# Shared-key attention with scores laid out by keys for the exponential and by queries for the maximum

## The reference

```
def gqa_attention(q, k, v):          # q, k were normed and rotated
    scale = HEAD_DIM ** -0.5
    def block(j, qb):
        logits = jnp.einsum("bqhgd,bkhd->bhgqk", qb, k).astype(jnp.float32) * scale
        p = jax.nn.softmax(logits, axis=-1).astype(v.dtype)
        return jnp.einsum("bhgqk,bkhd->bqhgd", p, v)
...
o = gqa_attention(q, concat([kc, k]), concat([vc, v]))     # 512 queries, 768 keys
oc = gqa_attention(qc, kc, vc) if need_ctx else None       # 256 queries, 256 keys; layer 0 only
x = x + gt * ((o * silu(z)) @ w_out)
```

## Time and profile before

| | us |
|---|---|
| median of 3 runs | 3264.06 |
| lowest and highest | 3261.76, 3265.40 |
| profiled execution, device time | 3259.84 |
| its span | 3258.0 |
| TensorE, VectorE, ScalarE, POOL busy | 3124.7, 1493.2, 1305.8, 1122.0 |
| granted TensorE clock, mean | 0.987 |

### The profile page before, as it was taken

One profiled execution on the slowest core, in us unless ns is written; L12 is line 12 of the kernel. 1 busy time (PEld: TensorE's weight loads), 2 busy tenths in 40 slices (PEclk: granted clock), 3 DMA queues, 4 the chain that ended last, 5 costly groups with the idle time before them and its releaser, 6 DMA issues. The chain is left out here.

```text
span 3258.0 us, 50609 instructions
## 1 busy us (share of the span) xinstructions
PE 3124.7 (96%) x20584; PEld 2577.8 (79%) x20584; DVE 1493.2 (46%) x2748; ACT 1305.8 (40%) x2383; POOL 1122.0 (34%) x614
## 2 busy tenths in 40 slices
PE   9989999999989999999999999999999998799999
PEld 7757788887667888888887888887888777688787
DVE  5952443218744344242476410246333349843473
ACT  4352333223533333232466213267223248723463
POOL 4532444446414444433111222242224422125212
PEclk9999999999999999999999999999999999999999
DMA  4355222324452323222000121110122200013102
GB/s 166 112 182 175 84 97 97 100 86 138 161 189 79 99 95 113 95 81 87 21 2 21 59 65 59 59 44 15 59 67 88 79 20 1 8 52 116 40 2 78
DMA packets 83878, 259.92 MB, mean 80 GB/s; under 512 B 11968, under 2 KB 17472, under 8 KB 83648
## 3 DMA queue, kind: packets, MB, share of 16 engines
q1 hardware_dynamic: 83648, 256.69, 23.8%
HBM read 239.34 MB, written 2.10 MB: 74 GB/s over the span
## 5 line engine op out<-in xcount | busy, mean ns | idle before, releaser
L188 PE MATMUL ps<-hs,head 128*128 128x512 f32 (+1 forms) x4176 | 864.3, 364 | 17.2 <-DVE hs L1068 6.8
L188 PE MATMUL ps<-hs,WS 128*128 128x512 f32 (+1 forms) x4176 | 855.1, 362 | 7.9 <-POOL WS L169 7.8
L188 PEld LDWEIGHTS ps<-hs,head 128*128 128x128 f32 x4176 | 711.9, 189 | 158.1 <-issue 13.4
L188 PEld LDWEIGHTS ps<-hs,WS 128*128 128x128 f32 x4176 | 710.6, 189 | 135.4 <-POOL WS L169 10.3
L169 POOL TENSOR_TENSOR WS<-W,WS 128x1024 fp32r<-128x1024 f32 x168 | 406.9, 2422 | 643.9 <-ACT WS L161 643.9
L169 POOL TENSOR_TENSOR head<-W,head 128x1024 fp32r<-128x1024 f32 x165 | 400.4, 2426 | 623.5 <-ACT head L161 623.5
L161 ACT CAST WS<-W 128x1024 fp32r<-128x1024 f32 x168 | 176.1, 1048 | 341.2 <-PE ps L188 315.1
L1846 ACT ACTIVATE prob<-ps,low 128x768 f32<-128x768 f32 (+4 forms) x320 | 223.6, 701 | 165.6 <-DVE low L1920 109.4
L161 ACT CAST head<-W 128x1024 fp32r<-128x1024 f32 x165 | 172.7, 1047 | 196.6 <-PE ps L188 196.5
L1355 PE MATMUL ps<-kk,qq 64*128 64x256 f32 (+3 forms) x2064 | 213.3, 333 | 25.8 <-ACT prob L1583 14.7
L1355 PEld LDWEIGHTS ps<-kk,qq 64*128 64x128 f32 x2064 | 156.5, 185 | 93.4 <-issue 41.4
(11 more groups left out here) (325 smaller groups left out, 3776.1 us busy)
## 6 DMA issues: line engine op xcount, KB each, us to landing
W<-in_stream_dram SPq DMA_DIRECT2D x433, 512.0 KB, 3.3
swap<-prj SPq DMA_DIRECT2D x168, 64.0 KB, 2.5
band<-in_bias_band_dram SPq DMA_DIRECT2D x8, 512.0 KB, 4.1
prj<-prj SPq DMA_DIRECT2D x64, 64.0 KB, 2.8
xT<-in_x_dram SPq DMA_DIRECT2D x4, 512.0 KB, 6.2
out_dram<-xT SPq DMA_DIRECT2D x8, 256.0 KB, 2.7
W<-in_stream_dram SPq DMA_DIRECT2D x1, 1536.0 KB, 10.9
xT<-in_ctx_dram SPq DMA_DIRECT2D x1, 1024.0 KB, 7.1
```

The source lines that it names most:

```text
L188: last = pe.matmul(out, a(i), b(j), start=start and n == 0, stop=stop and n == 2)
```

## The change

Only layers 0 and 3 take the new `attention_by_columns`. Work is now by steps: a step (g, j) is one block of 128 keys against the 512 queries of a pair. Scores are computed twice, with three products each. Once with keys on partitions (`score`): keys stationary, queries moving, and a fourth product that adds the negated maximum of each query (a matrix of ones times `shift`); the exponential of that can go as it is into the product with the values (`weigh`), with 512 columns moving. And once, a group ahead, with queries on partitions (`rank`), only to find the maximum (`largest`): 8 units of 128 queries and 384 keys, all in banks 0 and 1 after the first group. The maxima are turned once a group (`turn`) and laid out by `lay_shift`. Row sums are formed by POOL (the sum of two steps' probabilities, `pair`) and TensorE (`total`, ones in 32 columns, one strip of the array for each 128 queries), inverted by VectorE (`invert`, 128 x 128), spread by TensorE (`spread_inverse`) and applied by VectorE (`scale`) after the gate (`gate`). Context queries of two pairs form one group of 512 columns with two steps and two ranking units.

```
--- before.py
+++ after.py
@@ -1940,6 +1940,282 @@
+class Columns:
+    def __init__(self, groups):
+        self.groups = groups
+        self.steps = [(g, j) for g, (_, _, _, _, blocks) in enumerate(groups) for j in range(len(blocks))]
+        self.start = [0] + np.cumsum([len(blocks) for *_, blocks in groups]).tolist()
+        self.units_before = [0] + np.cumsum([len(self.units(g)) for g in range(len(groups))]).tolist()
+    def units(self, g):
+        n = len(self.groups[g][4])
+        return [(t, i) for t in range(4) for i in range(2)] if n == NT else [(0, 0), (2, 0)]
+    def units_at(self, g, j):
+        if g + 1 == len(self.groups):
+            return []
+        units, n = self.units(g + 1), len(self.groups[g][4])
+        at = range(1, n - 1) if n == NT else range(n)
+        return [u for i, u in enumerate(units) if at[i * len(at) // len(units)] == j]
+    def key_slot(self, g):
+        return self.groups[g][0] // 4
...
+def attention_by_columns(nc, M, C, operands, v_col, out, gate_tile):
...
+        prob, inv, sides = sb("prob", [P, 3, 2, S]), sb("inv", [P, P]), sb("sides", [P, 2, 32])
+        parts, low = sb("parts", [P, 2, 2, 4, 2]), sb("low", [P, 2, P])
+        pair = sb("pair", [P, 2, 2, S])
+        shift, ones, pick = sb("shift", [P, 2, S], F32R), sb("ones", [P, P], F32R), sb("pick", [P, 4])
...
+            @block.gpsimd
+            def _(pool):
...
+                for s, (g, j) in enumerate(steps):
+                    if j == 0 and g + 1 < G:
+                        pool.wait_ge(queries_high, g + 1)
+                        nc.gpsimd.tensor_tensor(place(q_at(g + 1, 1), g + 1), rows_of(M.prj, g + 1),
+                                                place(q_at(g + 1, 0), g + 1), ALU.subtract).then_inc(queries_low, 1)
+                    if s % 2:
+                        pool.wait_ge(exped, 2 * (s + 1))
+                        if s >= 5:
+                            pool.wait_ge(summed, s // 2 - 1)
+                        nc.gpsimd.tensor_tensor(pair[:, s // 2 % 2], prob[:, (s - 1) % 3], prob[:, s % 3], ALU.add
+                                                ).then_inc(paired, 1)
...
+            @block.tensor
+            def _(pe):
+                def rank(g, unit, bank):
+                    t, i = unit
+                    if len(groups[g][4]) == NT:
+                        pieces = [(0, t, 3 * P * i, 3 * P)]
+                    else:
+                        pieces = [(2 * P * x, t + x, S, 2 * P) for x in range(2)]
+                    for c, q, k, n in pieces:
+                        for x, (a, b) in enumerate(((0, 0), (1, 0), (0, 1))):
+                            for hd in range(2):
+                                last = pe.matmul(M.ps[:, bank + hd, c:c + n], q_at(g, a)[half(hd), q * P:(q + 1) * P],
+                                                 operands.kk[C.key_slot(g)][half(hd), b, k:k + n], start=x == 0,
+                                                 stop=x == 2)
+                    last.then_inc(ranked, 1)
+                def turn(g):
+                    if len(groups[g][4]) == NT:
+                        pe.wait_ge(lowered, g + 1)
+                    else:
+                        pe.wait_ge(maxed, C.units_before[g + 1])
+                    pe.transpose(M.ps[:, 0, 0:P], low[:, g % 2, :], M.const[:, C_ID:C_ID + P]).then_inc(turned, 1)
+                def score(s):
+                    g, j = steps[s]
+                    kb, kk = groups[g][4][j], operands.kk[C.key_slot(g)]
+                    if s >= 2:
+                        pe.wait_ge(exped, 2 * (s - 1))
+                    at = lambda hd: M.ps[:, 2 + 2 * (s % 2) + hd, :]
+                    for n, (a, b) in enumerate(((0, 0), (1, 0), (0, 1))):
+                        for hd in range(2):
+                            pe.matmul(at(hd), kk[half(hd), a, kb * P:(kb + 1) * P], q_at(g, b)[half(hd), :],
+                                      start=n == 0, stop=False)
+                    if j == 0:
+                        pe.wait_ge(shifted, g + 1)
+                    for hd in range(2):
+                        last = pe.matmul(at(hd), ones[half(hd), :], shift[half(hd), g % 2, :], start=False, stop=True)
+                    last.then_inc(scored, 1)
+                def weigh(s):
+                    g, j = steps[s]
+                    p, blocks = groups[g][0], groups[g][4]
+                    kb, first, final = blocks[j], j == 0, j == len(blocks) - 1
+                    pe.wait_ge(exped, 2 * (s + 1))
+                    if first and g:
+                        pe.wait_ge(gated, g)
+                    for hd in range(2):
+                        last = pe.matmul(M.ps[half(hd), 6, :], M.vtok[:, kb, v_col(p) + 64 * hd:v_col(p) + 64 * hd + 64],
+                                  prob[:, s % 3, hd, :], start=first, stop=final)
+                    last.then_inc(taken, 1)
+                def total(q):
+                    g, j = steps[2 * q]
+                    pe.wait_ge(paired, q + 1)
+                    if j == 0 and g:
+                        pe.wait_ge(scaled, g)
+                    for hd in range(2):
+                        for t in range(4):
+                            last = pe.matmul(M.ps[32 * t:32 * t + 32, 7, 0:P], sides[:, hd, :],
+                                             pair[:, q % 2, hd, t * P:(t + 1) * P], start=j == 0 and hd == 0,
+                                             stop=j == len(groups[g][4]) - 2 and hd == 1)
+                    last.then_inc(summed, 1)
+                def spread_inverse(g):
+                    pe.wait_ge(inverted, g + 1)
+                    for t in range(4):
+                        for hd in range(2):
+                            c = C_ID + 32 * t + 16 * hd
+                            last = pe.matmul(M.ps[half(hd), 7, t * P:(t + 1) * P],
+                                             M.const[:, c:c + 1].broadcast_to([P, 64]), inv[:],
+                                             start=True, stop=True)
+                    last.then_inc(spread, 1)
+                def sums(s):
+                    if s >= 3 and s % 2:
+                        total(s // 2 - 1)
+                    if s - 2 in C.start[1:]:
+                        spread_inverse(C.start.index(s - 2) - 1)
+                for n, unit in enumerate(C.units(0)):
+                    if n >= 3:
+                        pe.wait_ge(maxed, n - 2)
+                    rank(0, unit, 2 * (n % 3))
+                    keep_running(pe, M, 1, 7)
+                turn(0)
...
+                for s, (g, j) in enumerate(steps):
+                    score(s)
+                    n = len(groups[g][4])
+                    units = C.units_at(g, j)
+                    for unit in units:
+                        at = C.units_before[g + 1] + C.units(g + 1).index(unit)
+                        if unit == C.units(g + 1)[0]:
+                            pe.wait_ge(queries_low, g + 1)
+                            pe.wait_ge(shifted, g + 1)
+                            if g + 1 == second:
+                                pe.wait_ge(keys_low, 1)
+                        pe.wait_ge(maxed, at)
+                        rank(g + 1, unit, 0)
+                        if unit == units[0] and s:
+                            weigh(s - 1)
+                            sums(s)
+                    if not units:
+                        if j == n - 1 and n == NT and g + 1 < G:
+                            turn(g + 1)
+                        if s:
+                            weigh(s - 1)
+                            sums(s)
+                    if j == n - 1 and n < NT and g + 1 < G:
+                        turn(g + 1)
+                weigh(T - 1)
+                if T - 2 in C.start[1:]:
+                    spread_inverse(G - 2)
+                total(T // 2 - 1)
+                spread_inverse(G - 1)
...
+            def _(act):
...
+                    act.wait_ge(scored, s + 1)
+                    if s >= 3:
+                        act.wait_ge(taken, s - 2)
+                        act.wait_ge(paired, (s - 3) // 2 + 1)
+                    for hd in range(2):
+                        nc.scalar.activation(prob[:, s % 3, hd, :], M.ps[:, 2 + 2 * (s % 2) + hd, :], ACT.Exp
+                                             ).then_inc(exped, 1)
...
+                def largest(g, unit, bank):
+                    t, i = unit
+                    n = C.units_before[g] + C.units(g).index(unit)
+                    dve.wait_ge(ranked, n + 1)
+                    if len(groups[g][4]) == NT:
+                        dst, src = parts[:, g % 2, :, t, i], M.ps[:, bank:bank + 2, 0:3 * P]
+                    else:
+                        dst = low[:, g % 2, :].rearrange("p (h x) -> p h x", h=2)[:, :, t:t + 2]
+                        src = M.ps[:, bank:bank + 2, :].rearrange("p h (x n) -> p h x n", n=2 * P)
+                    v.tensor_reduce(dst, src, AX_X, ALU.max, negate=True).then_inc(maxed, 1)
```

(45 more changed lines are left out.)

46 lines of the change are left out of this document (added).

## The result

| | before | after |
|---|---|---|
| median, same chip | 3262.91 us (3258.34 to 3265.4, 4 runs) | 3402.05 us (3399.87 to 3404.39, 4 runs) |
| ratio, 95% interval | | 1.0421 [1.0409, 1.0434] |
| span of the profiled execution | 3258.0 | 3397.9 |
| layer 0's stage | 178.6 | 254.9 |
| layer 3's stage | 147.4 | 209.7 |

The change made the kernel 4.2% slower. A stage is taken here from the first load of its scores to the first load of the next stage. The two stages together grew from 326.0 to 464.6 us, 138.6 of the 139.9 us by which the spans differ. The rest of the program differs from execution to execution by some microseconds and is left alone. One execution of one variant took 4307 us at a mean granted clock of 0.74, in a slower state of the chip, and is left out of that variant's figures.

What follows compares the result with a forecast made beforehand. TensorE's streamed columns, changes of shape and waits for VectorE were taken as the bound: layer 3 +54.7, layer 0 +65.4, so 3259.8 + 120 = 3380, plus 4.2 to the median: 3384 us, range 3335 to 3430.

Steps and rivals of the forecast that it cites:

- The waits: TensorE idle for VectorE's reductions: 2.04 us behind the reciprocal, 1.86 behind the inverse's product, smaller ones; 5.68 a full group.
- A full group: Four works of a pair in layers 0 and 3: 19.70 us of TensorE plus waits, 25.4 against 17.55 before.
- rival 3: Totals: the four strips do not run together, 1.7 us instead of 0.43 each, time 3450; chance 0.05.
- rival 4: TensorE's clock falls to 1.2 GHz in the gaps, up to 17.5 us in each of 12 groups, up to 3594; chance 0.03.
- The start: Each stage's beginning: 10.0 us before the first block, with eight reductions in a row, then 18.3 for the rest of group 0.
- The contexts and the end: Layer 0's last part: three context groups of 11.1 us each, then 12.8 for the last one with the end.
- POOL's sum: Adding two blocks' probabilities: 2.42 us, up to 3.26; costed at nothing, with 8 us in all at the upper price.
- Rival 2: Weight loads are the bound in the two stages, fewer loads make the kernel faster, 3231 us; chance 0.03.
- The exchange: Per group on TensorE: 5.2 us of turning saved, spent on second scores (3.8), shift (1.3) and totals (1.3).
- 8R: Term for the eight ranking units' columns on TensorE in a full group: 4.32 us.
- Rival 1: VectorE's order costs nothing, reductions are done when ranking is due: 84 us less, 3300, still slower; chance 0.09.
- The signs: Expected profile after: groups of 25 us, reciprocal near 0.87, totals 0.43, VectorE near 50%, loads idle a fifth, clock 1.00.

Runs made afterwards that it cites:

- one ranking unit: Changed kernel with one of eight ranking units a full group kept, other maxima zero, queries scaled down 64 times: 3266.68 us, ratio 1.0008.
- reductions first: Changed kernel with VectorE taking the first reduction of each step before it gates, inverts or scales: 3339.8 us, ratio 1.0233.
- gaps filled: Changed kernel with three unread F32 matmuls of 256 columns put into each of the two long gaps of a full group: 3394.65 us, ratio 1.0397.
- one product in ranking: Changed kernel with the ranking maximum taken from the high-by-high product alone instead of three products: 3366.13 us, ratio 1.0302.

## Why the prediction was right, and where it was not

Forecast 3384, measured 3402: right in sign and inside the range, 18 us short. The mechanism, VectorE's order and the ranking chain, is what the experiments show; the nearness of the numbers is in part luck, as below.

- *The waits* came where they were listed, each released by a reduction. The loads' idle time of 2.16 and 1.90 us holds the change of shape too (0.20 and 0.17 where nothing is waited for), so 1.96 and 1.73 us compare with the sum's 2.04 and 1.86. TensorE started 0.05 us after VectorE's reduction (1632.37 + 0.90 = 1633.27, and 1633.32), not 0.15: the 0.14 of the earlier trace rows is ScalarE's. Taking the wait away by order alone gave 61 us of the 139.
- *A full group*: 25.4 forecast, 25.25 at full clock. The parts were less exact than the whole. The reciprocal took 0.96 us, not 0.87. The totals are 0.43 as forecast, so the strips run together and rival 3 is refuted, but I left out the change of shape between the product with the values and the totals, because no row of before had it. The Trainium skill, page "TensorEngine Tiling (Array Packing)", section Key Properties, has every change of tiling mode drain TensorE; the rows above agree, at 0.15 us. With 16 changes TensorE alone needs about 20.1 us, and the waits are 5.2, not 5.7 (20.1 is an estimate from the sum's prices). Two errors of half a microsecond cancelled; that the whole came out so near was luck.
- *The clock* was the largest error. I gave rival 4 a chance of 0.03, since gaps of 1.44 us had kept 1.00 and mine were to be "2.0". That reading was wrong as well: 1.44 is the idle time of the weight loads. In the start of layer 0's stage before, TensorE itself had nothing under way for 1.15 and 1.03 us:

```profile
1588.48 1.32 PE L1355 MATMUL ps<-kk,qq 64*128 64x512 f32 x12 [1.15 <-PEq L106]
...
1592.77 1.32 PE L1355 MATMUL ps<-kk,qq 64*128 64x512 f32 x12 [1.03 <-ACT prob L1846]
```

  The new gaps, measured the same way, are 1.89 and 1.66. The rival is partly what happened: in eight of twelve groups the clock fell for some microseconds, at 1.1 to 1.5 us each, 10 us in all. The fall is real, its price a twentieth of the rival's upper end.
- *The start*: 10.0 and 18.3 us forecast, 31.8 measured. I had the ranking units follow at the pace of the reductions; the unread matmul after each sets 1.36 us. The part to the end of the first scores took 13.5 us for 10.0, the rest of group 0 the 18.3 of the sum. That is 3.5 us a stage, and the term of the start is what was too small: the unread matmul stands in the change and was not counted.
- *The contexts and the end* took 49.4 us for the forecast 46.1: 12.0, 12.1 and 12.4 us for the three groups forecast at 11.1, and 12.8 as forecast for the last with the end. The clock falls in the second and third (they read 0.87 and 0.86), and in the first the ranking unit waits once for POOL, which has a sum of 2.38 us in front of the low part of the queries:

```profile
1799.04 2.38 POOL L2013 TENSOR_TENSOR pair<-prob 128x1024 f32<-128x1024 f32 x1 [3.18 <-ACT prob L2152]
...
1801.38 1.26 POOL L2007 TENSOR_TENSOR qq<-prj,qq 128x512 fp32r<-128x512 f32 x1
...
1802.69 0.77 PEld L2030 LDWEIGHTS ps<-kk,qq 64*128 64x128 f32 x12 [2.32 <-POOL qq L2007]
```

- Layer 0 then adds up: 3.5 + 4.1 (six groups, 156.5 for 152.4) + 0.2 (group 7, 17.1 for 16.9) + 3.3 = 11.1 of 11.2 us; layer 3 has 3.5 + 4.1 of 7.8.
- *POOL's sum* was 2.37 us in the mean, the lower bound, and no full group waited for it, as taken; the first context group did, which the sum had put at nothing.
- *Rival 2* is refuted: a group has fewer loads than before, their busy time is 11.5 of 25.25 us, from the 86% of the earlier trace rows, and the group became longer.
- *The exchange* of "5.2 us of columns" of turning for scores made twice was right in direction. (Its 3.8 for the second scores and 1.3 for the shift are columns at 2.4 GHz alone; the sum itself, which the forecast uses, has 8R = 4.3 and 1.4.) But it left out a bound. With five of six blocks not turned the works of before would take 4.29 us instead of 4.39, because of the ring through VectorE and ScalarE. The change does open that ring (one ranking unit: 16.24 us, all of it TensorE's), yet the chain of rank and reduce, which it puts in, is worse.
- *Rival 1*, 3300 if VectorE's order cost nothing, is refuted as a description of the change; as the worth of the order it was 84 us, and 61 were found; with the reductions first a group still has waits, such as the 0.68 us of loads shown above.
- *The signs*: groups every 25 us, totals and reciprocal came about as listed. VectorE was busy for 42% of a full group ("near 50%"), ScalarE for 28%. The loads stood idle for 54% of it, not for "a fifth", and the clock was not 1.00 throughout.

## What to carry to other kernels

Before you pay for removing an engine's work, see how long the ring through the other engines is that this work lies beside: here it was 4.29 us against 4.39, and the removal by itself was worth 0.3%. Work that only serves a number (a maximum, a bound) and feeds a single pair of banks makes a strict chain; on the engine that frees the banks, its step must stand first in the queue, ahead of work that waits for something else. A second pair of banks for ranking may loosen the chain too; no run tried it (the scores, the product with the values and the sums hold the other six). And when a shorter phase leaves the pitch between two units of it unchanged, the bound has moved to the engine that the wait names.

## What the hardware did that was not expected

- The granted clock fell to 0.50 in eight of the twelve full groups of the changed kernel, each time 0.1 to 1.5 us after the idle stretch of step 1, in which TensorE had nothing under way for 1.89 us (in group 1 the stretch ends at 1633.32 and the clock reads 0.50 from 1634.00 to 1636.70), and was back within the same group. It never fell after the stretch of step 2, 1.66 us. The same stretch did not always do it: four groups of twelve kept 1.00. In reductions first and gaps filled the longest such stretch in a full group was 0.34 and 0.40 us, and all groups read 1.00.
- With one product in ranking it fell more often (eleven groups against eight, one execution each). There it also read 0.50 from 1596.4 to 1609.6, in the start of layer 0, where the same instructions read 1.00 in another execution.
- Each change of the matmuls' shape cost 0.14 to 0.17 us where the pitch less the columns could be read: 64 rows to 128, 128 to 64, and 64 columns to 32.
- VectorE's reciprocal of 128 x 128 from PSUM took 956 to 958 ns, more than the longer forms of the earlier trace rows had led to (0.87 us).
